# Routed heads: the first unit's rows gathered feature-major by 32 products, with the split token rows as the stationary operand

## The reference

```python
logits = (h @ w_router).astype(jnp.float32)
top_vals, top_idx = lax.top_k(logits, TOP_K)
...
for e in range(N_EXPERTS):
    y = _swiglu(h, w_gate[e], w_up[e], w_down[e])
    out = out + gates[..., e:e + 1].astype(h.dtype) * y
```

## Time and profile before

| what | us |
|---|---|
| median of 3 runs | 2141.84 (2141.72, 2141.84, 2145.21) |
| profiled execution, device time | 2141.92 |
| its span, first to last instruction | 2140.1 |
| PE busy | 2076.6 (97%) |
| PEld busy | 1699.9 (79%) |
| DVE busy | 1700.9 (79%) |
| ACT busy | 1418.4 (66%) |
| POOL busy | 130.3 (6%) |
| PE's share of the chain that ended last | 84% |
| DVE's share of that chain | 9% |
| granted TensorE clock, mean | 0.996 |
| one copy of a weight piece to gu_hi on ACT (L1671), mean | 1.05 |
| one load of an activation table on ACT (L1831) | 1.28 |

### The profile page before, as it was taken

The page is one execution under the profiler, slowest core; times in us unless marked ns, Lnnn a source line. Parts: engine busy times, 40 slices in busy tenths (PEclk is TensorE's granted clock), DMA queues, the critical chain, the costliest instruction groups (busy, mean ns, idle before and its releaser), DMA issues.

```text
span 2140.1 us, 30894 instructions
## 1 busy us (share of the span) xinstructions
PE 2076.6 (97%) x10092; PEld 1699.9 (79%) x10092; DVE 1700.9 (79%) x2276; ACT 1418.4 (66%) x1889; POOL 130.3 (6%) x122
## 2 busy tenths in 40 slices
PE   8999999999998999999999999999999999999998
PEld 7876787867887887887776888888888888888887
DVE  4755998747997657445776999999999999999997
ACT  5662785444784634444442888888888888888885
POOL 1000100001000001111110100000000000000000
PEclk9999999999999999999999999999999999999999
DMA  7317895426993455551342799999999999999995
GB/s 274 135 75 288 338 410 203 163 97 243 412 382 113 183 219 214 200 200 72 137 177 99 316 379 387 371 382 384 368 390 377 385 374 389 374 382 378 366 403 204
DMA packets 88342, 601.59 MB, mean 281 GB/s; under 512 B 10336, under 2 KB 10400, under 8 KB 19776
## 3 DMA queue, kind: packets, MB, share of 16 engines
q1 hardware_dynamic: 79744, 570.40, 67.7%
q0 software_dynamic: 8512, 30.05, 4.7%
HBM read 585.11 MB, written 15.30 MB: 281 GB/s over the span
## 4 chain that ended last, share of the span: by engine, by line
PE 84%; DVE 9%; ACT 2%; DMA 2%; issue 2%; POOL 0%; DVEq 0%; SPq 0%; ACTq 0%
PE bank L503 24%; PE bank L505 24%; PE bank L504 24%; PE bank L1034 2%; PE bank L1494 2%; DVE gu_lo L1856 1%; PE bank L630 1%; DMA ffw_gu<-in_gate_up_m 1%; PE bank L2968 1%; DVE small L395 1%; DVE dn_lo L1856 1%; DMA pieces<-in_pieces 1%; PE bank L1536 1%; DVE pj_lo L540 1%; PE bank L444 0%
## 5 line engine op out<-in xcount | busy, mean ns | idle before, releaser
L1856 DVE TENSOR_TENSOR gu_lo<-ffw_gu,gu_hi 128x1024 fp32r<-128x1024 f32 x620 | 754.7, 1236 | 93.1 <-ACT gu_hi L1671 78.7
L1671 ACT CAST gu_hi<-ffw_gu 128x1024 fp32r<-128x1024 f32 x620 | 649.2, 1052 | 85.1 <-PE bank L505 44.3
L503 PE MATMUL bank<-gu_hi,xg_lo 128*128 128x512 f32 x1152 | 461.3, 400 | 0.0
L505 PE MATMUL bank<-gu_hi,xg_hi 128*128 128x512 f32 x1152 | 450.5, 391 | 0.0
L504 PE MATMUL bank<-gu_lo,xg_hi 128*128 128x512 f32 x1152 | 449.6, 390 | 0.0
L1856 DVE TENSOR_TENSOR dn_lo<-ffw_d,dn_hi 128x1024 fp32r<-128x1024 f32 x299 | 365.5, 1230 | 26.4 <-ACT dn_hi L1679 17.1
L1679 ACT CAST dn_hi<-ffw_d 128x1024 fp32r<-128x1024 f32 x310 | 326.5, 1056 | 63.1 <-PE bank L505 56.0
L503 PE MATMUL bank<-dn_hi,hidt_lo 128*128 128x512 f32 x664 | 260.0, 392 | 6.6 <-DVE hidt_lo L1856 6.4
L505 PE MATMUL bank<-dn_hi,hidt_hi 128*128 128x512 f32 x664 | 258.5, 389 | 0.0
L504 PE MATMUL bank<-dn_lo,hidt_hi 128*128 128x512 f32 x664 | 258.4, 389 | 0.0
L505 PEld LDWEIGHTS bank<-gu_hi,xg_hi 128*128 128x128 f32 x1152 | 216.2, 188 | 45.8
(11 more groups left out here) (442 smaller groups left out, 2688.3 us busy)
## 6 DMA issues: line engine op xcount, KB each, us to landing
ffw_gu<-in_gate_up_m SPq DMA_DIRECT2D x288, 1024.0 KB, 7.3
ffw_d<-in_down_m SPq DMA_DIRECT2D x144, 1024.0 KB, 8.9
pieces<-in_pieces SPq DMA_DIRECT2D x70, 1024.0 KB, 7.1
ffw_gu<-in_gate_up_ff SPq DMA_DIRECT2D x22, 1024.0 KB, 7.0
ffw_d<-in_down_ff SPq DMA_DIRECT2D x11, 1024.0 KB, 8.8
h<-token_sums POOLq DMA_DIRECT2D x3, 1024.0 KB, 7.0
pieces<-in_pieces SPq DMA_DIRECT2D x4, 512.0 KB, 8.0
norm_vec<-in_ln_g POOLq DMA_DIRECT2D x4, 512.0 KB, 4.5
```

Of the source, the lines that this page charges most:

```text
L503: nc.tensor.matmul(bank, a_lo, b_hi, start=start, stop=False)
L505: return nc.tensor.matmul(bank, a_hi, b_hi, start=False, stop=stop)
L1671: nc.scalar.copy(gu_hi[:, 2 * k:2 * k + 2, :], ffw_gu[:, blk["slot"], 2 * k:2 * k + 2, :])\
L1856: return V.tensor_tensor(out, x, hi.bitcast(F32), ALU.subtract)
```

## The change

- `gather_tensor` no longer makes token-major rows. For each of the 8 feature chunks, for the high and the low parts of the token rows, and for both token tiles, it issues one product: stationary is the chunk of the token rows (128 tokens by 128 features, taken with a stride of 8 elements), moving is `pick_t` (128 columns). These are 32 products. They leave the high parts feature-major in banks 5 and 6 and the low parts in banks 2 and 3. `rows_turned` is signalled after 16 and after 32 products.
- `row_x_scalar`, the 8 turns of the first unit and the filler on both sides of them are gone.
- `rows_hi_scalar` copies banks 5 and 6 as before; it now waits for products instead of turns.
- `first_rows_lo_vector` takes the place of the first `rows_lo_vector`: a plain copy of banks 2 and 3 to `xg_lo`, which no longer waits for ACT. It stands ahead of `slot_index_vector` instead of behind it.
- The exponent on ACT moves behind both `xg_hi` copies, and the table of Exp is loaded explicitly ahead of them.
- PE waits for the rows half by half: the first pair of weight pieces needs only chunks 0 to 3.

```diff
--- before.py
+++ after.py
@@ -1517,22 +1517,20 @@
     def gather_tensor(pe, t):
 
         pe.wait_ge(sem("pick_ready"), 2 * ROUTER[t] + 1)
-        for half in range(2):
-            cols = slice(half * 512, (half + 1) * 512)
-            for j in range(T):
-                for part, src in enumerate((tok_lo, tok_hi)):
-                    last = nc.tensor.matmul(psum[5 + half], pick_t[:, j, :], src[:, j, cols],
-                                            start=(j == 0 and part == 0), stop=(j == T - 1 and part == 1))
-            last.then_inc(sem("gathered"), 1)
+        for c in range(DC):
+            for bank, src in ((5, tok_hi), (2, tok_lo)):
+                for j in range(T):
+                    last = nc.tensor.matmul(psum[bank + c // 4][:, (c % 4) * P:(c % 4 + 1) * P],
+                                            src[:, j, :].rearrange("t (p c) -> t c p", c=DC)[:, c, :], pick_t[:, j, :],
+                                            start=(j == 0), stop=(j == T - 1))
+            if c % 4 == 3:
+                last.then_inc(sem("rows_turned"), 1)
 
     def rows_turn_tensor(pe, t, u):
 
         for c in range(DC):
             if c == 0:
-                if isinstance(u, int) and u == 0:
-                    pe.wait_ge(sem("row_x_ready"), 2 * ROUTER[t] + 2)
-                else:
-                    pe.wait_ge(sem("rows_fetched"), 16 * (FFS[t][2] - ROUTER[t] + u))
+                pe.wait_ge(sem("rows_fetched"), 16 * (FFS[t][2] - ROUTER[t] + u))
             last = nc.tensor.transpose(psum[5 + c // 4][:, (c % 4) * P:(c % 4 + 1) * P],
                                        row_x.rearrange("t (p c) -> t c p", c=DC)[:, c, :], ident)
             if c % 4 == 3:
@@ -1645,12 +1643,10 @@
         keep_busy_tensor(1, 5 if t == "m2" else 3)
         pe.wait_ge(sem("tok_ready"), T * (ROUTER[t] + 1))
         gather_tensor(pe, t)
-        keep_busy_tensor(1, 4)
-        rows_turn_tensor(pe, t, 0)
-        keep_busy_tensor(1, 8)
-        pe.wait_ge(sem("rows_split"), 2 * q0 + 2)
         st = make_step(t, 0, 0, 0)
         for pair in range(2):
+            pe.wait_ge(sem("rows_hi_ready"), 2 * q0 + pair + 1)
+            pe.wait_ge(sem("rows_split"), 2 * q0 + pair + 1)
             gate_up_tensor(pe, st, x_of(0), pair)
         pe.wait_ge(sem("first_gates"), ROUTER[t] + 1)
         permute_tensor(pe, sem("permuted"))
@@ -1700,12 +1696,6 @@
         act.wait_ge(sem("down_piece"), DOWN_PIECES * (st["s"] - 1) + DOWN_USED)
         nc.scalar.copy(hidT_hi[:, st["par"]].rearrange("p f t -> p (f t)"),
                        psum[2][:, st["par"] * BLK:(st["par"] + 1) * BLK]).then_inc(sem("hidt_hi_ready"), 1)
-
-    def row_x_scalar(act, t):
-
-        for half in range(2):
-            act.wait_ge(sem("gathered"), 2 * ROUTER[t] + half + 1)
-            nc.scalar.copy(row_x[:, half * 512:(half + 1) * 512], psum[5 + half]).then_inc(sem("row_x_ready"), 1)
 
     def rows_hi_scalar(act, q, side):
         for k in range(2):
@@ -1788,9 +1778,6 @@
             for j in range(T):
                 ins = nc.scalar.activation(scaled[:, j, :], h[:, j, :], ACT.Copy, scale=ALPHA)
             ins.then_inc(sem("h_scaled"), 1)
-        act.wait_ge(sem("route_masked"), ROUTER[t] + 1)
-        nc.scalar.activation(r_e, r_e, ACT.Exp).then_inc(sem("route_exp"), 1)
-
         def unit(u, side, final):
             q = q0 + u
 
@@ -1826,8 +1813,10 @@
                 return
             step(make_step(t, u + 1, 0, 0), last, make_step(t, u + 1, 0, 1))
             sums_copy_scalar(act, t, u, last)
-        row_x_scalar(act, t)
+        nc.scalar.preload_act_table(ACT.Exp)
         rows_hi_scalar(act, q0, 0)
+        act.wait_ge(sem("route_masked"), ROUTER[t] + 1)
+        nc.scalar.activation(r_e, r_e, ACT.Exp).then_inc(sem("route_exp"), 1)
         nc.scalar.preload_act_table(ACT.Silu)
         begin(make_step(t, 0, 0, 0), make_step(t, 0, 0, 1))
         units(act, t, unit)
@@ -1909,6 +1898,12 @@
             dve.wait_ge(sem("rows_hi_ready"), 2 * q + k + 1)
             rest(lo[:, 4 * k:4 * k + 4, :].rearrange("p c t -> p (c t)"), psum[5 + k],
                  hi[:, 4 * k:4 * k + 4, :].rearrange("p c t -> p (c t)")).then_inc(sem("rows_split"), 1)
+
+    def first_rows_lo_vector(dve, t):
+        lo = xg[0][1]
+        for k in range(2):
+            dve.wait_ge(sem("rows_turned"), 2 * FFS[t][2] + k + 1)
+            V.tensor_copy(lo[:, 4 * k:4 * k + 4, :].rearrange("p c t -> p (c t)"), psum[2 + k]).then_inc(sem("rows_split"), 1)
 
     def row_gate_vector(dve, t, u, s):
         n = FFS[t][4] if FFR[t] else 1
@@ -2286,8 +2281,8 @@
         if grouped:
             best_two()
             exponents()
+        first_rows_lo_vector(dve, t)
         slot_index_vector(t)
-        rows_lo_vector(dve, FFS[t][2], 0)
         vlink(V.tensor_scalar(r_sum[:, 0], r_sum[:, 0], SLOTS + 0.5, None, ALU.is_gt))
         vlink(V.tensor_copy(flags[:, ROUTER[t]:ROUTER[t] + 1], r_sum[:, 0]), sem("route_flag"))
         dve.wait_ge(sem("route_exp"), ROUTER[t] + 1)
```

## The result

| | median, us | span of the profiled execution, us | mean clock |
|---|---|---|---|
| before | 2141.78 (2140.60 to 2145.21) | 2140.1 | 0.996 |
| after | 2155.20 (2153.22 to 2155.95) | 2153.0 | 0.987 |

The ratio is 1.0064, 95% interval 1.0052 to 1.0075: **slower by 13.4 us**, where 2.5 us faster was forecast. It lies outside the range and beyond the slow rival's 2149.0. Two runs in the chip's slower state, 2332.9 us of the kernel before and 4231.28 us of the changed one, are left out of every median here.

A forecast was written before the change was run, and what follows sets the result against it. DVE's arrival at the row gate (L1922) in the three heads was taken as the bound. Gains of 13.66 - 93p, 2.50 us at p = 0.120 us a product, gave 2139.3 us; the range ran from 2136.0 to 2145.0.

The forecast's parts named there:

- the slow rival: Gather products: a narrow fp32r product costs what plain fp32 does, 0.224 us, giving 2149.0 us; chance 15%.
- DVE's way to the row gate: Heads: when DVE reaches L1922 sets the time, its lead passing one to one to PE and the loads.
- the rule in p: Gain to L1922: 4.90 - 31p in m0 and m1, 3.86 - 31p in m2; sum 13.66 - 93p us.
- p: Pace of the 32 gather products: taken as 0.120 us each, bounds 0.060 and 0.224.
- PE's wait for `hidt_lo`: Behind the m0 and m1 heads: PE, 3.0 us ahead, waits about 2 us in all for gu_lo and hidt_lo.
- the rival by which PE's lead counts: Heads: PE's lead, not DVE's, sets the time; 7.7 us gained, 2134.1 us; chance 3%.
- the turns show that neither the stride nor 128 columns changes much: Gather products: turns with the same strided stationary operand, 0.127 us a step, were used to support 0.120 us a product.
- The upper bound of 0.224: Gather products: at most 0.224 us each, from plain fp32 fillers of 128 columns, two records at 0.112 us.
- turning point of 0.147 us: Gather products: the pace at which the forecast gain turns into a loss, 13.66 / 93.
- moving it is free: ACT's exponent behind the xg_hi copies: done at 211.6, needed at about 213.3, 1.7 us to spare.
- the forecast's 1.18 us: First two heads: DVE reaches L1922 at 219.03 instead of 220.21, credited to the whole change.
- SyncE's load 1.2 us forward: Behind the head: L2017, the fourth weight block's load, was to be issued 1.2 us sooner, following DVE.

The follow-up runs named there:

- stride taken away: Changed kernel with the stationary operand taken as 128 neighbouring features instead of every eighth, so features reach the experts in the wrong order: 2139.09 us in one execution.
- 256 columns: Changed kernel with 24 of the 32 products given pick_t twice, 256 moving columns, the second copy being overwritten: 2152.07 us, ratio 1.0052.
- second profile: The changed kernel itself, unaltered, measured again beside the others on the same chip: 2154.36 us, ratio 1.0058.
- the first experiment: Changed kernel with both operands of the 32 products read as plain fp32, two records a product: 2174.26 us, ratio 1.0159.
- the kernels with contiguous weights: Changed kernel with chunks of 128 neighbouring features and gate-and-up weights laid out to match, without and with slot_index ahead of the low rows in m2: 2142.28 and 2140.74 us.
- the weights by chunk: Changed kernel with chunks of 128 neighbouring features and the routed layers' gate-and-up weights laid out to match: 2142.28 us, ratio 1.0001.
- the index first: Changed kernel with neighbouring-feature chunks and matching gate-and-up weights, plus slot_index ahead of the low rows in the third head: 2140.74 us, ratio 0.9994.
- the run with mixed strides: Changed kernel with chunks 0 to 7 of the stationary operand at strides 1, 2, 3, 4, 8, 16, 8, 1: 2150.05 us in one execution.

## Why the prediction was wrong

**Right: DVE's way to the row gate as the measure, and the rule in p.** Forecast against measured change of that stretch, m0 / m1 / m2 in us:

| p | rule | measured |
|---|---|---|
| 0.111 (stride taken away) | +1.46 / +1.46 / +0.42 | +1.34 / +1.33 / +0.30 |
| 0.2415 (256 columns, clock 1.00) | -2.59 / -2.59 / -3.63 | -2.79 / -2.79 / -3.83 |
| 0.2415 (after, clock falls) | -2.59 / -2.59 / -3.63 | -3.32 / -3.12 / -3.87 |
| 0.2415 (after, second profile, clock falls) | -2.59 / -2.59 / -3.63 | -2.81 / -2.81 / -3.85 |

Wherever the clock is up, the rule is 0.1 to 0.2 us too kind. PE's wait for `hidt_lo` of about 2 us with a fast gather came as said (1.68 us), and the rival by which PE's lead counts is out. What the rule doesn't cover is the way between the heads, where the stretches at half clock move a profile by 0.8 to 2.0 us each; that the run with contiguous products comes out at 2139.09, near the rule's 2138.6 at 0.111, is in part luck, for 1.2 of its span's 3.1 us lie ahead of m0.

**Wrong: p, and with it the sign.** The step that failed is the sentence "the turns show that neither the stride nor 128 columns changes much". The columns indeed change little (strided 0.24 us with 128 and with 256; contiguous 0.111 and 0.120). But the turns are transposes, and their loads pay 0.052 us for the stride where a product's pay 0.145. By the rule the difference of 0.12 us is 93 x 0.1215 = 11.3 of the 15.9 us by which the forecast is off; of the rest, 0.6 us is the rule's kindness, up to 0.9 the clock in the heads, and the remainder lies between the heads. The trace of before held a warning, in the groups of the weight loads:

```profile
L1494 PEld LDWEIGHTS bank<-ident,arena 128*128 128x128 f32 x332 | 45.9, 139 | 22.4 <-DVE arena L1881 0.7 <-DVE arena L1884 0.3
...
L1536 PEld LDWEIGHTS bank<-ident,arena 128*128 128x128 f32 x128 | 15.5, 192 | 2.6 <-ACT arena L1708 2.6
```

Turns of unstrided tiles load in 0.139 us, strided ones in 0.192. I went by the distance of starts, where 0.127 us seemed harmless, and not by the load behind it. The upper bound of 0.224 was taken from plain fp32 with a contiguous operand, so it did not bound the stride at all; a bound for an access pattern that no product of the trace has should have been wider. The Trainium skill, "TensorE: Matmul & The Clock Gate", section "LDWEIGHTS (loading the stationary operand)", lets the load depend on the number of columns alone; the runs show 0.192 and 0.337 us for the same 128.

**Right sign, wrong cause: the slow rival.** It had the sign, and its turning point of 0.147 us lies between the paces of a gain and of a loss (0.111 and 0.24); no run is near it. Its cause, the type, is refuted by the first experiment: the same pace per record in either type. The Trainium skill, "TensorE: Matmul & The Clock Gate", section "Back-to-back issue gap", gives about 81 ns for 128 columns; the fastest products of these runs with 128 columns and contiguous operands are 111 ns apart.

**Missed: the clock.** I had no rival on it. Its fall in the heads costs 0.1 to 0.9 us inside them. The medians (2.3 and 3.1 us above the 256-column kernel's) allow more of the 13.4, but don't show it.

**Mis-sized: the exponent.** I wrote that moving it is free. It is the part that brings the forecast's 1.18 us in m0 and m1; the 32 products at their best add 0.6 us over the three heads. The parts should have been priced one by one from the kernel before.

**Missed: who else uses the DMA queues.** I moved SyncE's load 1.2 us forward and POOL's read-back 0.6 us, and did not ask which was first. The order turns in the changed kernel already (in m0 of the first profile, in both heads of the second); with fast products it takes back up to 1.6 us of the 2.7 that m0 and m1 gain.

**Open: the whole time of the kernels with contiguous weights.** Of the roughly 3 us by which the two kernels with contiguous weights miss their heads' promise, the collision is a part. Another 0.3 us lies outside the span: device time less span is 2.09 us for the changed kernel and its relatives, 1.78 for the kernel before. A further 1.0 us goes in the third layer, from the row gate to the end: 956.18 and 956.22 us in the profiles of these two, 955.14 before and 955.22 with the stride alone taken away; why is open. The clock over the whole run takes part too. Of the 29 runs of before beside these two kernels, the six with a mean clock of 0.997 took 2139.25 to 2140.64 us and the two with 0.994 took 2143.91 and 2145.11, an estimate from these of 1.5 us for each 0.001. The mean over all runs is 0.9956 before, 0.9953 with the weights by chunk and 0.9944 with the index first, so by this estimate some 0.5 and 1.8 us. No run takes these parts from each other.

The fastest kernel of the study that computes the reference is the kernel before with the exponent moved, 2.2 and 2.8 us or 0.1% below it in two sets of runs, each with an interval that reaches 1.0.

## What to carry to other kernels

Before an operand is made stationary, look at its stride in elements: price the product from the weight-load rows with the same stride and the same kind of operation, not from a neighbour's pace, and take a transpose for no stand-in for a product. Price each edit of a bundle alone on the kernel before, since here the small one carried the gain and the large one the loss. When the order of a head changes, list the transfers that move and those that don't, and see whether their order turns. And before a difference of 1 or 2 us between two traces is put down to an edit, lay the stretches at half clock of both beside each other.

## What the runs showed of the hardware

- The stationary load of a 4-byte product at full clock: 0.192 us at stride 1, 0.337 at stride 8, and products 0.111 and 0.24 us apart; the distance is 0.117 at stride 2, 0.175 at 3, 0.233 at 4, and 0.22 at 16 at half clock. Stride 8 costs the same in fp32r and per record of fp32, for 128 and 256 moving columns, and at half clock. Why a turn's load pays so much less (0.140 to 0.191) is open.
- Source reads with a stride of 8 elements: ACT's copy of 128 x 1024 takes 2.12 us instead of 1.05, DVE's pair of subtractions 4.00 instead of 2.36.
- The clock fell to 0.50 behind 128-column fp32r products 0.24 us apart with PE recorded as busy throughout, in all three heads of both profiles of the changed kernel; in the profiles with 256 columns or with two fp32 records per product, just as far apart, it was 1.00 in all three. It fell in all three heads of the run with mixed strides as well. What sets it off wasn't tried further.
- A 16 KB read on POOL's queue in the first two heads landed 5.3 to 5.9 us after its issue when 2 MB of weights had been issued 0.3 to 1 us ahead of it on another queue, and 1.9 to 2.1 us after it otherwise. The profile of the changed kernel has both: 5.48 us in m0, where the load came 0.29 us first, and 1.92 in m1, where it came 0.64 us later.
